# Two-layer diffusion backbone on one core: modulation rows loaded and reduced tile by tile in two half buffers

## The reference, cut to what matters

```python
mx = (jax.nn.silu(c) @ w_mod[l] + b_mod[l]).reshape(B, N_MOD, 1, D)        # N_MOD = 9 groups of 1024
mc = (jax.nn.silu(c_ctx) @ w_mod[l] + b_mod[l]).reshape(1, N_MOD, 1, D)
x = x + 0.5 * mx[:, 2] * swiglu(modulate(rms_norm(x), mx[:, 0], mx[:, 1]), w_gate, w_up, w_down)
...
def swiglu(h, w_gate, w_up, w_down):
    return (jax.nn.silu(h @ w_gate) * (h @ w_up)) @ w_down                  # 1024 -> 2816 -> 1024
```

## Time and profile before

| what | us |
|---|---|
| median of 3 runs (2893.99 to 2897.52) | 2895.42 |
| the profiled execution, its own time | 2897.35 |
| its span, first to last instruction | 2895.5 |
| PE busy in the span | 2738.1 |
| DVE busy | 1913.8 |
| ACT busy | 1180.5 |

### The profile page before, as it was taken

One profiled execution on the slowest core, in us unless ns is written; L12 is line 12 of the kernel. 1 busy time (PEld: TensorE's weight loads), 2 busy tenths in 40 slices (PEclk: granted clock), 3 DMA queues, 4 the chain that ended last, 5 costly groups with the idle time before them and its releaser, 6 DMA issues.

```text
span 2895.5 us, 40323 instructions
## 1 busy us (share of the span) xinstructions
PE 2738.1 (95%) x15679; PEld 2564.4 (89%) x15679; DVE 1913.8 (66%) x3239; ACT 1180.5 (41%) x2080; POOL 262.8 (9%) x279
## 2 busy tenths in 40 slices
PE   7999999989988899999999999999999998999999
PEld 5999999979977789999999999898988987878887
DVE  5786868764477757868675678786665587553333
ACT  4242424343378742424243434242443388422222
POOL 1000000022224210000000100000012234000000
PEclk9999999999999999999999999999999999999999
DMA  6333333232100223333331322424223102243333
GB/s 226 99 103 116 117 117 117 89 84 61 48 14 9 74 73 106 106 117 117 111 94 52 99 85 88 144 84 149 62 62 94 50 14 54 83 143 96 98 98 95
DMA packets 305899, 263.95 MB, mean 91 GB/s; under 512 B 11119, under 2 KB 283925, under 8 KB 304689
## 3 DMA queue, kind: packets, MB, share of 16 engines
q1 hardware_dynamic: 304176, 256.86, 29.1%
q10 hardware_dynamic: 896, 4.46, 0.4%
q0 software_dynamic: 640, 0.09, 0.0%
HBM read 255.08 MB, written 2.10 MB: 89 GB/s over the span
## 4 chain that ended last, share of the span: by engine, by line
PE 70%; DVE 13%; DMA 6%; ACT 5%; issue 4%; POOL 1%; SPq 0%; DVEq 0%; ACTq 0%; POOLq 0%
PE pair L489 9%; PE pair L490 9%; PE pair L497 9%; PE pair L1138 7%; PE pair L1140 7%; PE pair L1139 7%; DVE pmid L1019 5%; DMA d_raw<-in_w_ffn_down 4%; PE pair L1779 2%; PE pair L1781 2%; PE pair L1780 2%; PE pmid L2582 2%; DVE xT L1582 1%; PE pair L752 1%; PE psum L1140 1%
## 5 line engine op out<-in xcount | busy, mean ns | idle before, releaser
L489 PE MATMUL pair<-s_six,d_tile 128*128 128x384 f32 x984 | 340.1, 346 | 42.7 <-ACT d_tile L1084 25.5
L489 PE MATMUL pair<-h_lo,w_hi 128*128 128x512 f32 (+2 forms) x928 | 332.9, 364 | 6.8 <-ACT w_hi L458 6.0
L490 PE MATMUL pair<-s_six,d_tile 128*128 128x384 f32 x984 | 337.5, 343 | 0.0
L1019 DVE SCALAR_TENSOR_TENSOR pmid<-mod_raw,cs_rows 128x1024 f32<-128x1024 f32 x256 | 314.3, 1228 | 27.8 <-DMA mod_raw<-in_w_mod_rows 24.7
L490 PE MATMUL pair<-h_hi,w_hi 128*128 128x512 f32 (+2 forms) x928 | 331.4, 363 | 0.0
L1582 DVE SCALAR_TENSOR_TENSOR xT<-pair,mv,xT 128x384 f32<-128x384 f32 (+5 forms) x312 | 143.1, 508 | 190.2 <-PE pair L497 186.0
L489 PEld LDWEIGHTS pair<-s_six,d_tile 128*128 128x128 f32 x984 | 191.7, 195 | 48.7 <-ACT d_tile L1084 29.6
L1294 ACT ACTIVATE p_hi<-p_raw 128x512 fp32r<-128x512 f32 x270 | 167.7, 628 | 149.9 <-DVE p_raw L1324 52.6
L1138 PE MATMUL pair<-h_lo,p_hi 128*128 128x384 f32 x648 | 218.2, 337 | 10.8 <-ACT sg L1339 10.8
L1084 ACT ACTIVATE d_tile<-d_raw 128x768 fp32r<-128x768 f32 (+1 forms) x96 | 76.0, 791 | 372.3 <-DMA d_raw<-in_w_ffn_down 220.3
L1138 PE MATMUL pair<-t_lo,p_hi 128*128 128x384 f32 x648 | 217.9, 336 | 4.9 <-DVE sg L1346 3.3
(11 more groups left out here) (377 smaller groups left out, 6462.6 us busy)
## 6 DMA issues: line engine op xcount, KB each, us to landing
mod_raw<-in_w_mod_rows SPq DMA_DIRECT2D x64, 1024.0 KB, 5.1
p_raw<-in_w_ffn_gate SPq DMA_DIRECT2D x27, 1024.0 KB, 7.4
p_raw<-in_w_ffn_up SPq DMA_DIRECT2D x27, 1024.0 KB, 5.4
d_raw<-in_w_ffn_down SPq DMA_DIRECT2D x72, 384.0 KB, 5.9
w_raw<-in_w_ffn_gate SPq DMA_DIRECT2D x34, 512.0 KB, 3.9
w_raw<-in_w_ffn_up SPq DMA_DIRECT2D x34, 512.0 KB, 3.8
w_raw<-in_w_in SPq DMA_DIRECT2D x32, 512.0 KB, 4.0
w_raw<-in_w_ffn_down SPq DMA_DIRECT2D x16, 512.0 KB, 4.1
```

What stands on the lines that cost most here:

```text
L489: eng.matmul(dst, wh, rl, start=k == 0, stop=False)
L490: eng.matmul(dst, wh, rh, start=False, stop=False)
L1019: eng.scalar_tensor_tensor(pmid[:, 0:D_MODEL], mod_raw[:, a, :], 1.0, cs_rows[:, j, :], ALU.mult, ALU.mult, accum_out=mod[:, 2 * v + a, j: ...
```

## The change

Each tile of `w_mod` now has a half of `mod_raw` and a semaphore of its own (`mod_loaded[m % 2]`), is loaded by a transfer of 512 KB, and its load waits for the two dots of the tile before last. Dots are planned one by one (`DOT_PLAN`, in the order of `DOT_ORDER`), and the load that a finished tile allows is queued at the place of the tile's second dot, behind weight loads. Dots an FFN: 96, 96, 64, 0 (96, 72, 72, 16 before). In stages 1 to 3 of inst 0 and 1 a group part has 16 dots (12 before, none in inst 1's stage 3), with two instead of one ahead of `pair_lo` 4 of group (1, 1) and ahead of the last `pair_mul` of group (2, 1), and the down part 11 or 10 on tiles 0 to 5 (16 before in stages 1 and 2, four of them on tile 7; 12 in inst 0's stage 3, none in inst 1's); in inst 2 a group part has 13. The loads of down tiles and of the next stage's first gate and up blocks are moved in SP's queue. Of the token work, sums 6 and 7 and all `token_hi` and `token_lo` move: sum 6 ahead of the wait for the last up tile, the rest to down tiles 0 to 4. The first group's weight preparation in `ff_dve` is spread otherwise over down tiles 5, 6 and 7.

```diff
+PAIR_PLACES = [(p, up, h) for p in range(3) for up in range(2) for h in range(2)] + [(2, 1, 2)]
+def _dot_plan():
+    up = {("up", 0, i, h): 2 for i in range(4) for h in range(2)}
+    six = lambda s, more: {("pair", s) + at: 1 + (at in more) for at in PAIR_PLACES}
+    down = lambda s, counts: {("down", s, d): n for d, n in enumerate(counts)}
+    full, part = ((1, 1, 1), (2, 1, 1), (2, 1, 2)), ()
+    plan = [{**up, **six(1, full), **six(2, full), **six(3, full),
+             **down(1, (2, 2, 2, 2, 2, 1, 0)), **down(2, (2, 2, 2, 2, 2, 1, 0)), **down(3, (2, 2, 2, 2, 2))} for _ in range(2)]
...
+        def mod_load(eng, m):
+            n = m - START_MOD
+            if n >= 2:
+                eng.wait_ge(mod_step, 2 * (n - 1))
+            l, at = divmod(m, MOD_TILES)
+            src = w_mod_rows[l].rearrange("(t p) k -> p t k", p=P)[:, at, :]
+            eng.dma_start(mod_raw[:, m % 2, :], src).then_inc(mod_loaded[m % 2], 16)
+        def mod_loads(eng, inst, *place):
+            for n in dots_at(inst, place):
+                if n % 2 and n // 2 + 2 < dots_before(inst + 1) // 2:
+                    mod_load(eng, START_MOD + n // 2 + 2)
+        def mod_dots(eng, inst, *place):
+            for n in dots_at(inst, place):
+                m, j = START_MOD + n // 2, n % 2
+                if j == 0:
+                    eng.wait_ge(mod_loaded[m % 2], (n // 4 + 1) * 16)
...
-                for i in range(KD // 2):
-                    planned_load(eng, inst, ("down", s, i))
-                    if i == 0 and inst < 3 and 0 < s and not last_stage:
...
+                for d in range(KD):
+                    if d == 0 and inst < 3 and 0 < s and not last_stage:
                         pair_load(eng, inst, s + 1, 0, 0)
+                    if d + 4 < KD:
+                        ff_down_load(eng, inst, s, d + 4)
+                    if d == KD - 3 and inst < 3 and not last_stage:
+                        eng.wait_ge(w_lo_done, down_tile(inst, s, KD - 1)[0].n(1))
+                        pair_load(eng, inst, s + 1, 0, 1)
+                    mod_loads(eng, inst, "down", s, d)
...
-                    if inst < 3 and i == st["n"] - 1:
-                        for b in range(2):
-                            token_lo(eng, inst, b)
...
+                    if inst < 3 and s == 0:
+                        if d == 0:
+                            token_sums(eng, inst, (7,))
+                        elif d < 5:
+                            token_lo(eng, inst, d - 1)
```

More of the change, by code:

```diff
@@ L986, in mod_turn, with dots_before, dots_at, first_mod_loads @@
             last.then_inc(mod_turned, 1)
[L988 to L994, removed]
-            src = w_mod_rows[l].rearrange("(t a p) k -> p t a k", p=P, a=2)[:, at, :, :]
-            eng.dma_start(mod_raw[:, :, :], src).then_inc(mod_loaded, 16)
+        def dots_before(inst):
+            return sum(sum(DOT_PLAN[n].values()) for n in range(inst))
+        def dots_at(inst, place):
+            first = dots_before(inst)
+            for at in DOT_ORDER:
+                if at == place:
+                    break
+                first += DOT_PLAN[inst].get(at, 0)
+            return range(first, first + DOT_PLAN[inst].get(place, 0))
+        def mod_load(eng, m):
[5 more added lines that the diff above has]
+            eng.dma_start(mod_raw[:, m % 2, :], src).then_inc(mod_loaded[m % 2], 16)
+        def first_mod_loads(eng, inst):
+            for m in range(2):
+                mod_load(eng, START_MOD + dots_before(inst) // 2 + m)
+        def mod_loads(eng, inst, *place):
+            for n in dots_at(inst, place):
+                if n % 2 and n // 2 + 2 < dots_before(inst + 1) // 2:
+                    mod_load(eng, START_MOD + n // 2 + 2)
         def cs_spread_out(eng, j):
@@ L1234, in first_loads @@
             if b[:2] == "ff":
-                ff_up_load(eng, int(b[2]), 0, 0)
+                for j in range(2):
+                    ff_up_load(eng, int(b[2]), 0, 0, j)
             else:
@@ L1247, in ff_sp @@
                     if i + 1 < st["n"]:
-                        ff_up_load(eng, inst, s, i + 1)
+                        for j in range(2):
+                            ff_up_load(eng, inst, s, i + 1, j)
+                            if i and inst < 3:
+                                mod_loads(eng, inst, "up", s, i - 1, j)
                     else:
@@ L1561, in ff_act @@
                         out_copy(eng, d - 1)
-                    if inst < 3 and s == 0 and d in (1, 3):
-                        token_hi(eng, inst, 2 + d // 2)
+                    if inst < 3 and s == 0 and d < 4:
+                        token_hi(eng, inst, d)
                     if crossing:
@@ L1599, in ff_dve @@
                         next_lo(eng, inst, s, 2 * i + 2)
-                    for j in range(2):
-                        planned_dot(eng, inst, ("up", s, i), 0, j)
+                    mod_dots(eng, inst, "up", s, i, 0)
+                    if inst < 3 and i == 3:
+                        token_sums(eng, inst, (6,))
                     eng.wait_ge(acc_done, o.n(2))
@@ L1711, in turn_bank @@
             return BANKS[(TURN_AT[l][u] - TURN_AT[l][0] + b) % 4]
-        def mod_pairs_through(inst):
-            return PAIR_0 + sum(len(plan) for plan in MOD_PLAN[:inst + 1])
-        def mod_pairs_before(l):
-            return mod_pairs_through(2 * l) - PAIR_0
         def latent_product(eng, t, dst, a, d):
```

146 lines of the change are left out of this document (62 added, 84 removed).

## The result

| | us |
|---|---|
| kernel before, median of 4 runs (2893.74 to 2897.52) | 2894.70 |
| changed kernel, median of 4 runs (2812.52 to 2815.28) | 2812.93 |
| ratio, with its 95% interval | 0.9718 [0.9701, 0.9734] |
| the profiled execution: its own time, its span | 2815.28, 2813.5 |

The span is 82.0 us shorter than before. The page's engine line shows where: PE has 27 us less of busy time (less of it at the low clock) and 55 us less of waits; DVE's sum is nearly that of the earlier trace rows, 3.5 us more.

The account below looks back on a forecast made before the run. PE, busy 2738 of 2895 us, and its waits make the time. Gains 20.3 + 54.2 + 12.3 + 10.0 less 14.5 give 82.3 us: 2897.35 becomes 2815.0, and with that run 1.9 above the median, 2814; range 2797 to 2842.

Parts of the forecast that it names:

- Middle: Stage 1's down part to stage 3's groups, three FFNs: 883.7 falls to 829.5 without waits, 54.2 us gained before penalties.
- stage 0's down parts: Stage 0, three FFNs: token work moved from ahead of tile 0's `residual` takes 123.8 to 103.5, 20.3 us gained.
- last down part, inst 0 and 1: Inst 0's 67.48 us comes to 55.2 with loads ahead of dots, 12.3 gained; inst 1 gets dots at no cost.
- first group parts, inst 0 and 1: Stage 1's group parts, where a second dot in group (1, 1) costs PE all of its 1.32 us.
- inst 3: Product 0 to product 6 falls from 75.34 to 65.3 us without dots, 10.0 gained.
- SP's queue: First cause: down tile loads issued behind a pair's load that waits for four dots; PE waits 25.5 us, 13 times.
- The halves: 0: 128 transfers for 64, same bytes: longer transfer time is covered and nothing waits, so 0 us.
- Four dots on the last tile: Third cause: four dots on the last down tile, 5.3 us, push back the first group's preparation and the `up` block's load.
- The second dots: Ends of groups (1, 1) and (2, 1): 1.32 and 1.1 us, together 2.4, in three stages of two FFNs: -14.5.
- free: Rival, 0.12: PE's seven products have slack, so the second dots cost nothing and the time is 2800 us.
- DVE the bound: Rival, 0.13: in group parts four added dots cost PE 5.3 us in full and lower the clock: 2842 us.
- The queue of `p_raw`: Rival, 0.03: slower than before, as `p_raw` blocks behind half loads come late in every group; 2927 at 2.5 us each.

Follow-up runs that it names:

- the one with both moved: Changed kernel with the second dots moved from the ends of groups (1, 1) and (2, 1) to those of (1, 0) and (2, 0): 2796.51 us, 0.9653.

## Why the prediction was right, and where its reasons were not

The time, 2812.93 for 2814, is right, and term by term the stretches agree. "Middle" is from stage 1's down part to stage 3's groups; the price of the second dots, 1.3 a group part and 1.1 a down part, is taken off where it falls:

| term | predicted | measured |
|---|---|---|
| stage 0's down parts | 20.3 | 123.81 - 103.22 = 20.6 |
| middle, with its part of the penalties | 54.2 - 9.7 = 44.5 | 883.65 - 838.49 = 45.2 |
| last down part, inst 0 and 1 | 12.3 - 2.2 = 10.1 | 12.4 - 1.2 = 11.2 |
| first group parts, inst 0 and 1 | -2.6 | -1.4 twice = -2.8 |
| inst 3 | 10.0 | 75.34 - 65.25 = 10.1 |

The right column adds up to 84.3, the span fell by 82.0. The other 2.3 us went the other way in stretches that the sum left out, 0.8 of them in inst 2's last down part (54.12 before, 54.91 now).

- **Stage 0** was right in mechanism and size; undone, it costs 17.
- **SP's queue** was right as the cause of the 25.5 us: mended alone it brings the down parts to 49.92 each. What the prediction didn't see is that the wait had two supports. No wait was longer than 2.8 us, and whole loads ahead of the down tiles were 2.6 us of the lateness. In the changed kernel, with halves, the old order costs 6 to 9.
- **"The halves: 0"** is the step that failed. It asked only whether a half would be waited for, and not what the whole loads cost already. Alone in the kernel before the halves are worth 26.6: they take the down loads up to 2.6 us forward, and in inst 3 let a row's load go out while the other row is still being read. In the changed kernel undoing them costs 36.8, by a third way: the new plan puts dots that follow each other on both sides of a pair's border, in groups and in down parts. The total came out since all this sits in stretches that I had compared with clean ones: the sum said what would be left when nothing waits, not which edit would do it. 46.2 and 26.6 can't be added: six down parts had 37.3 us over clean ones (336.83 against 299.52), of which the queue takes all and the halves 31.0. No kernel had just these two.
- **Inst 3**: right in size, wrong in cause. "One step is 10.89 where no dot is" is true, but the dots fit into the step. The cost was DVE's wait for a whole load, 4.78 us in the row of the kernel before shown above, and what followed from it: without the dots there, and with the dots and halves, the 10 us are gone.
- **Four dots on the last tile** stood in the prediction as the third cause, without a size of its own, and its step "which push the first group's preparation back" is wrong. In the kernel before, the last `pair_lo` of the first group are done as the dots begin (302.25, to 307.4, in inst 0's stage 2). What is late behind them is DVE's first sum for the second group, by the same chain as with four dots put back:

```profile
308.09 0.63 ACT L1294 ACTIVATE p_hi<-p_sum 128x512 fp32r<-128x512 f32 x1 [3.99 <-DVE p_sum L1314]
308.62 0.47 ACT L1339 ACTIVATE sg<-pair 128x384 f32<-128x384 f32 x1
```

  Where the queue alone was mended, the group parts behind the dots stand 15.6 us over clean ones, those without a wait (543.89 against six times 88.05), the most that the dots can have cost there; put back into the changed kernel they cost 29. One difference shows in inst 0's stage 2: there the dots begin 4.4 us into the group for 3.3, since tile 7 now has more of the preparation ahead of them, and the fourth waits 1.13 us for its half.
- **The second dots** cost 17.2 for 14.5 by medians, and 16.4 by the windows of the changed kernel and of the one with both moved: 8.2 in six group parts (1.4 each for 1.3), 5.2 in four down parts (1.3 for 1.1) and 3.0 in two last down parts. 8.9 + 3.7 us are waits that the changed kernel shows at these places. The chain DVE, ACT, PE at the end of (1, 1) was read rightly from the earlier trace rows. The rival "free" would have shown none of the six waits, and "DVE the bound" would have shown its cost wherever the dots stand: it went with the place.
- **The queue of `p_raw`** (the rival on the slow side) never came near: PE has no wait for `p_lo` or `p_hi`, and DVE none for a load of `mod_raw`.
- **The slow stretches.** The prediction counts 14 behind the 22 waits of the earlier trace rows and uses that against DVE as the bound. The trace has 10 behind those; the other four are behind other waits, two in inst 0's last down part and two in inst 3. The total doesn't hang on it, since the sum compares stretches.

On 512 KB transfers the Trainium skill, "DMA: Bandwidth & Descriptors", section "Bandwidth", asks for 1 MiB and more. The profile's row bears out the price in transfer time: 128 halves at 3.6 us are 461 us, 64 pairs at 5.1 were 326. By that rule the changed kernel would be slower with halves; the runs decide the other way, by 27 and 37 us.

```profile
mod_raw<-in_w_mod_rows SPq DMA_DIRECT2D x128, 512.0 KB, 3.6
```

What stays open: whether the old queue would cost more than 6 to 9 us in the changed kernel without its second dots, where PE comes to tile 4 earlier, was not tried; nor the old queue and whole loads together on the new plan.

## What to carry to other kernels

A transfer behind another on an in-order queue inherits the other's wait and its size; look at both, since either may be the microsecond that makes it late, and mending one hides the other (the two down tiles of the earlier trace rows landed 6.2 us behind their issue with 1024 KB just ahead, 5.1 with 512 KB, and 3.5 is the median of the changed kernel). The size of a transfer into a buffer is also the grain in which the buffer comes free: where an engine reads it piece by piece between work that others wait for, load it piece by piece. Extra work on an engine that is 76 of 88 us busy can cost nothing or all of itself, by the instruction that it stands ahead of: look there for who waits, and move it by one group.

## What the runs showed of the hardware

The low clock stood mostly behind PE's longer waits. Behind each of the twelve waits of 0.6 to 1.5 us at the second dots it stayed full: PEclk 1.00 in inst 0's first group part and in all middle windows of the changed kernel (the 0.97 of inst 1's last down part belongs to a later wait there, see below). Behind the six waits of 3.1 to 3.2 us with the halves alone it fell to 0.50, that is 1.2 GHz; here right behind the one that ended at 305.6 of inst 0:

```profile
306.69:310.10 3.41, 3.41 (x13) 3.41 (x12) 2.87 (x6) 1.75 (x4) 0.00 (x0) 0.50 0.92 314
```

It is why a wait of 1.5 us at a second dot costs a group part no more than 1.4, and a wait of twice that some 1.7 us beyond itself (half of 3.41, an estimate). But the length of the wait alone doesn't decide. Near the end of the last down part of the changed kernel PE waits 1.5 us in inst 0, where PEclk stays 1.00, and the same 1.5 us in inst 1, where it fell behind it (0.97 in the window). Of three waits of 3.0 us at one place with four dots on the last tile, two kept 1.00 (windows of 92.67 us) and one did not (92.84, 0.98). The 2.4 us of inst 2's stage 0 with the old token order kept 1.00 too. What decides between them is not shown.
